# Thirty-two tokens out of the dense expert tiles, and up products with the weights stationary behind all down products

## What is computed

```python
q = (hblk @ w_q).reshape(B, TB, PEER_HEADS, 2, PEER_DHALF)
s = jnp.einsum('btphd,phnd->btphn', q, subkeys)
v, i = lax.top_k(s, PEER_TOPK)                       # 16 of 128 in each half
cand = v[..., 0, :, None] + v[..., 1, None, :]
cidx = i[..., 0, :, None] * PEER_NKEYS + i[..., 1, None, :]
tv, tj = lax.top_k(cand, PEER_TOPK)
eidx = take_along_axis(cidx, tj)
w = jax.nn.softmax(tv, axis=-1)
a = jax.nn.gelu(einsum('btd,btpkd->btpk', hblk, w_down[eidx]))
y = einsum('btpk,btpkd->btd', w * a, w_up[eidx])
x = x + ga2 * y;  out = rms_norm(x, g_norm_final)
```

## Time and profile before

| | us |
|---|---|
| median of three runs | 1717.1 (1715.06 to 1717.36) |
| the profiled execution | 1716.91 |
| its span, first to last instruction | 1715.6 |
| first route step starts on TensorE | 1099.95 |
| last of the 64 route steps ends | 1331.3 |
| the ten pairs end | 1384.4 |
| last up product ends | 1708.8 |
| TensorE busy, share of the span | 98% |
| VectorE busy | 77% |
| ScalarE busy | 56% |
| GpSimd busy | 15% |

### The profile page before, as it was taken

The page is one execution under the profiler, slowest core; times in us unless marked ns, Lnnn a source line. Parts: engine busy times, 40 slices in busy tenths (PEclk is TensorE's granted clock), DMA queues, the critical chain, the costliest instruction groups (busy, mean ns, idle before and its releaser), DMA issues.

```text
span 1715.6 us, 30262 instructions
## 1 busy us (share of the span) xinstructions
PE 1674.8 (98%) x10348; PEld 1496.5 (87%) x10348; DVE 1314.5 (77%) x2590; ACT 956.2 (56%) x1779; POOL 255.6 (15%) x204
## 2 busy tenths in 40 slices
PE   9999999999999999999899999999999999999998
PEld 8888888799988887889899999999989888888886
DVE  5468877867788788867668787799999776666667
ACT  5746554466555544657445554588888543333333
POOL 2120000012100000321117793100010000000000
PEclk9999999999999999999999999999999999999999
DMA  7534767656547677444245558766655555556554
GB/s 241 185 134 154 260 213 273 220 169 211 200 148 274 209 281 257 160 157 144 87 130 193 170 198 310 241 197 196 193 188 168 190 193 190 193 195 195 189 192 146
DMA packets 91674, 336.53 MB, mean 196 GB/s; under 512 B 10305, under 2 KB 10673, under 8 KB 90801
## 3 DMA queue, kind: packets, MB, share of 16 engines
q1 hardware_dynamic: 77328, 279.48, 49.3%
q0 software_dynamic: 7040, 30.20, 5.2%
q10 hardware_dynamic: 7200, 25.45, 3.9%
HBM read 332.94 MB, written 2.13 MB: 195 GB/s over the span
## 4 chain that ended last, share of the span: by engine, by line
PE 52%; DVE 12%; DMA 5%; ACT 4%; issue 3%; POOL 1%; DVEq 0%; SPq 0%; ACTq 0%; POOLq 0%
PE bank L282 12%; PE bank L286 12%; PE bank L283 12%; PE bank L1259 4%; DMA ring<-in_stream 4%; DVE wl L208 4%; ACT wh L201 3%; PE bank L2368 2%; PE bank L1263 2%; PE bank L2371 1%; DVE onehot_j L2686 1%; DVE x L2614 1%; DVE gelu L2387 1%; DVE onehot_i L2685 1%; DMA ada<-in_w_ada 1%
## 5 line engine op out<-in xcount | busy, mean ns | idle before, releaser
L201 ACT ACTIVATE wh<-ring 128x1024 fp32r<-128x1024 f32 x526 | 555.5, 1058 | 560.4 <-PE bank L286 376.6
L208 DVE TENSOR_TENSOR wl<-ring,wh 128x1024 fp32r<-128x1024 f32 x476 | 582.0, 1225 | 274.1 <-ACT wh L201 272.3
L282 PE MATMUL bank<-wh,xs 128*128 128x512 f32 (+1 forms) x852 | 307.6, 361 | 1.9 <-DVE wl L208 0.8
L286 PE MATMUL bank<-wh,xs 128*128 128x512 f32 (+1 forms) x852 | 303.7, 356 | 0.0
L283 PE MATMUL bank<-wl,xs 128*128 128x512 f32 (+1 forms) x852 | 303.4, 356 | 0.0
L282 PE MATMUL bank<-xs,wh 128*128 128x224 f32 (+1 forms) x760 | 214.8, 283 | 4.4 <-DVE wl L208 4.1
L1259 PE MATMUL bank<-xs,wh 128*128 128x512 f32 x672 | 212.4, 396 | 2.5 <-DVE wl L208 2.5
L286 PE MATMUL bank<-xs,wl 128*128 128x224 f32 (+1 forms) x760 | 211.3, 278 | 0.0
L283 PE MATMUL bank<-xs,wh 128*128 128x224 f32 (+1 forms) x760 | 211.2, 278 | 0.0
L2368 PE MATMUL bank<-xs,wh 128*128 128x448 f32 x592 | 189.7, 382 | 0.0
L282 PEld LDWEIGHTS bank<-wh,xs 128*128 128x128 f32 x852 | 160.9, 189 | 28.1 <-DVE wl L208 2.9
(11 more groups left out here) (529 smaller groups left out, 2780.2 us busy)
## 6 DMA issues: line engine op xcount, KB each, us to landing
ring<-in_stream SPq DMA_DIRECT2D x529, 512.0 KB, 3.4
ada<-in_w_ada ACTq DMA_DIRECT2D x48, 512.0 KB, 4.6
rows<-in_rows POOLq DMA_DIRECT2D x1, 2560.0 KB, 11.4
rows<-in_rows POOLq DMA_DIRECT2D x3, 512.0 KB, 5.5
con<-in_early POOLq DMA_DIRECT2D x1, 1374.0 KB, 14.4
x_feature_major<-in_x_fm SPq DMA_DIRECT2D x4, 256.0 KB, 6.3
x<-in_x_tm POOLq DMA_DIRECT2D x1, 1024.0 KB, 5.8
rows<-in_rows POOLq DMA_DIRECT2D x1, 1024.0 KB, 7.0
```

The source lines that it names most:

```text
L201: C.activation(wh[q % AHEAD][:, :], ring[slot][:, :], ACT.Copy).then_inc(s_high, 1)
L208: low.tensor_tensor(wl[q % AHEAD][:, :], ring[slot][:, :], wh[q % AHEAD][:, :], ALU.subtract).then_inc(s_low, 1)
L282: T.matmul(o, left[0], right[0], start=start, stop=False, skip_group_check=True)
L286: return T.matmul(o, left[1], right[0], start=False, stop=stop, skip_group_check=True)
```

## The change

The three groups of edits are these.

- The thirty-two tokens leave the dense work wholly. `ROUTES` falls to 56, `WA` has 224 columns. For their up part, 32 more gathers fetch up rows, from the stream itself. `take_row` is one instruction on DVE for each gathered row set: 32 dots, then (after `factors`: gelu of the dots, times the routing weights) 32 multiply-adds into `own`, which becomes the tokens' result spread over 128 partitions. Takes come in every fifth route step, every third down step behind the routes and every third up step, 64 in all, with two buffers. 16 small matmuls sum over the heads at the end. `x` stays in SBUF.
- `FIRST` falls from 54 to 39, and all downs come before all ups: 39 lead, 56 with a route step, 33 wide downs alone, then 128 ups.
- An up is weight-stationary in the form of the wide down: eight blocks of a matmul with 448 columns and one with 224, into eight PSUM banks. The high part of the weighted activations is made by ACT, the low part by DVE. The result lies by feature, so it is scaled by `ga2` per partition (`result_block`, which also adds the two sides) and transposed back on TensorE before the sum with `x`.

```diff
-FIRST = 54
+FIRST = 39
-BUFS = 3
+BUFS = SETS
-BY_POOL = 28
-ROUTES = S // TB
-LEAD = FIRST + ROUTES
+BY_POOL = 30
+ROUTES = LIVE // TB
+DOWNS = NE - FIRST
+BESIDE_UP = 3
```

```diff
+    def take_row(n):
+        row, r = rows_of[n % BUFS][:, :], n % DOTS
+        mine = own[r // TOPK][:, :]
+        V.wait_ge(s_row[n % BUFS], 16 * (n // BUFS + 1))
+        if n < DOTS:
+            V.tensor_tensor_reduce(out=row, in0=row, in1=mine, ..., accum_out=dots[:, r:r + 1]).then_inc(s_taken, 1)
+        elif r % TOPK == 0:
+            V.tensor_scalar(mine, row, dots[:, r:r + 1], None, ALU.mult).then_inc(s_taken, 1)
+        else:
+            V.wait_ge(s_taken, n)
+            V.scalar_tensor_tensor(mine, row, dots[:, r:r + 1], mine, ALU.mult, ALU.add).then_inc(s_taken, 1)
```

The order of a step with a down tile, in the changed form:

```diff
+    for g in range(DOWNS):
+        if g < ROUTES:
+            route_product(g)
         down_wide(q1 + g, 0, FIRST + g, 0)
         if g + 1 < ROUTES:
             weights_in(g + 1)
         if g >= 1:
             late_gelu(g - 1)
+        if 1 <= g <= ROUTES:
             route_copy(g - 1)
+        if 2 <= g < ROUTES + 2:
             route_multiply(g - 2)
         if g >= 3:
             late_weigh(g - 2)
         if g + 2 < ROUTES:
             onehots(g + 2)
         split(q1 + g + AHEAD)
         late_whole(g)
+        if g % 5 == 2 if g < ROUTES else (g - ROUTES) % 3 == 0:
+            take_row(taken)
+            taken += 1
+    late_gelu(DOWNS - 1)
```

And the ups:

```diff
+    def parts(u):
+        if u >= 3:
+            C.wait_ge(s_used, q2 + u - 2)
+        C.activation(parts_of(u)[:, 0, 0:LIVE], WA[:, u, :], ACT.Copy).then_inc(s_high_part, 1)
+        V.wait_ge(s_high_part, u + 1)
+        V.tensor_tensor(parts_of(u)[:, 1, 0:LIVE], WA[:, u, :], parts_of(u)[:, 0, 0:LIVE], ALU.subtract).then_inc(s_parts, 1)
+    def up_block(u, k, h, l):
+        def both_parts(stop):
+            return T.matmul(sides(k)[:, :, 0:LIVE], h[:, ks], hold[:, :, 0:LIVE], ...)
+        def high_part(stop):
+            return T.matmul(bank[k][:, 0:LIVE], l[:, ks], hold[:, 0, 0:LIVE], ...)
+    for u in range(NE - LATE):
+        up(u)
+        if u + 2 < NE:
+            parts(u + 2)
+        if q2 + u + AHEAD < pieces:
+            split(q2 + u + AHEAD)
+        if u % BESIDE_UP == 1 and taken < 2 * DOTS:
+            if taken == DOTS:
+                factors()
+            take_row(taken)
+            taken += 1
+    parts(NE - 1)
+    T.wait_ge(s_taken, 2 * DOTS)
+    for i in range(SETS):
+        for k in range(KD):
+            T.matmul(sides(k)[:, :, toks], own[i][:, k * P:(k + 1) * P], spread[:, :, :], start=False, stop=True, ...)
+    for k in range(KD):
+        for v in range(LATE):
+            last = up_block(u, k, wh[q % AHEAD], wl[q % AHEAD])
+        if k == 6:
+            for b_ in range(4):
+                result_block(b_)
+            turned_back(0, 0)
+            turned_back(1, 0)
```

More of the change, by code:

```diff
@@ L2292, in build @@
     peer = ExitStack()
-    WA = sb(peer, "weighted", [P, NE, S])
+    WA = sb(peer, "weighted", [P, NE, LIVE])
+    own = [sb(peer, f"own_rows{i}", [P, D]) for i in range(SETS)]
+    rows_of = [sb(peer, f"gathered{i}", [P, D]) for i in range(BUFS)]
     iT = sb(peer, "route_i", [P, S])
@@ new lines, in factors @@
+    def factors():
+        C.wait_ge(s_taken, DOTS)
+        made = act.did(C.activation(dots[:, :], dots[:, :], ACT.Gelu_apprx_tanh))
+        dve.wait(made)
+        V.wait_ge(s_wts_in, 16)
+        made = dve.did(V.tensor_tensor(dots[:, :], dots[:, :], wts[:, :], ALU.mult))
+        V.wait_ge(*made)
+    V.wait_ge(*picked)
+    m = dve.did(V.scalar_tensor_tensor(ups_f, IJ[:, 1, 1].rearrange("p h k -> p (h k)"), float(NE),
+                                       IJ[:, 0, 1].rearrange("p h k -> p (h k)"), ALU.mult, ALU.add))
@@ L2641, in build @@
+    V.wait_ge(*m)
+    numbered_up = dve.did(V.tensor_scalar(ups_of, ups_f, float((pieces - NE) * P), None, ALU.add))
+    V.memset(spread[:, 1, :], 0.0)
+    spread_made = dve.did(V.tensor_reduce(spread[:, 0, :], ident.rearrange("p (t h) -> p t h", h=PH), AX.X, ALU.add))
     act.wait(s1)
@@ L2939, in last_tile @@
-    def last_tile(v, i):
-        n = 0 if i is None else i * BODY
-        u, q = NE - LEAD + v, q2 + v
-        if i is not None or u + 2 < NE:
-            parts(u + 2, n, q, n, last=True)
-        up(q, n, u, n, last=i is not None or v > 0)
-        if i is not None or q + AHEAD < pieces:
-            split(q + AHEAD, i)
-    V.wait_ge(s_weighed, NE - LEAD)
-    parts(NE - LEAD + 1, 0, q2 - 1, 0, last=True)
-    for v in range(BODY):
-        last_tile(v, None)
-    with nc.Fori(1, LEAD // BODY - 1, engines=(ENG.PE, ENG.Activation, ENG.DVE)) as i:
-        for v in range(BODY):
-            last_tile(v, i)
@@ L2955, in build @@
-    ga2_diag = WA[:, 12:16, :].rearrange("p j (a n) -> p (j a) n", a=2)
-    dg2 = diagonals(ga2_diag, 5 * KD)
-    for v in range((LEAD // BODY - 1) * BODY, LEAD - 3):
-        last_tile(v, None)
-        if v == LEAD - 4:
-            ga2, ga2_done = row_of(WA[:, 16:20, :].rearrange("p j t -> p (j t)"), ga2_diag, dg2)
-    parts(NE - 1, 0, q2 + LEAD - 3, 0, last=True)
-    order = [(0, 0, 0), (0, 0, 1), (1, 0, 0), (2, 0, 0), (1, 0, 1), (2, 0, 1), (0, 1, 0), (1, 1, 0), (2, 1, 0),
-             (0, 1, 1), (1, 1, 1), (2, 1, 1)]
@@ new lines, in up @@
+    def up(u):
+        T.wait_ge(s_parts, u + 1)
+        def products(h, l):
+            for k in (0, 1, 2, 3, 7, 4, 5, 6):
+                if u == 0 and k == 0:
+                    T.wait_ge(s_wc, ROUTES)
+                    T.wait_ge(s_wm, ROUTES)
+                if u == 0 and k == 4:
+                    T.wait_ge(s_whole, DOWNS)
+                last = up_block(u, k, h, l)
+            return last
+        piece_ops(q2 + u, 0, products)
+    for u in range(2):
+        parts(u)
+    late_weigh(DOWNS - 2)
@@ new lines, in build, with result_block @@
+    for i in range(SETS):
+        toks = slice(LIVE + i * GROUP, LIVE + (i + 1) * GROUP)
+        for k in range(KD):
+            T.matmul(sides(k)[:, :, toks], own[i][:, k * P:(k + 1) * P], spread[:, :, :], start=False, stop=True,
+                     skip_group_check=True)
+    result = flat[:, 7168:9216].rearrange("p (k t) -> p k t", k=KD)
+    right = flat[:, 9216:10240].rearrange("p (i t) -> p i t", t=S)
+    block_done, right_in, block_in, summed_up = {}, {}, {}, {}
+    def result_block(k):
+        col = mod[:, 5 * KD + k:5 * KD + k + 1]
+        act.wait(block_done[k], block_in.get(k - 4))
+        right_in[k] = act.did(C.activation(right[:, k % 4, :], bank[k][:, S:2 * S], ACT.Copy, scale=col))
+        V.wait_ge(*right_in[k])
+        block_in[k] = dve.did(V.scalar_tensor_tensor(result[:, k, :], bank[k][:, 0:S], col, right[:, k % 4, :], ALU.mult, ALU.add))
```

346 lines of the change are left out of this document (119 added, 227 removed).

## The result

| | before | after |
|---|---|---|
| median of seven runs each, us | 1715.06 (1711.76 to 1717.36) | 1704.67 (1700.52 to 1708.48) |
| ratio after / before | | 0.9939, 95% interval 0.9925 to 0.9954 |
| the profiled execution, us | 1716.91 | 1708.48 |
| its span | 1715.6 | 1707.2 |
| first route step starts | 1099.95 | 1052.05 |

The kernel got 10.4 us faster, where 23 were forecast: the sign was right, but more than half of the gain is missing.

The account below looks back on a forecast made before the run. TensorE, busy for 98% of the span, was taken to bound the kernel. Start of the routes -46.9, route steps -31.9, downs and pairs +47.5, ups with their ends +7.0, tail +1.1 gave 1694 us, range 1679 to 1713.

Parts of the forecast that it names:

- The ring between ACT and DVE: In the lone downs, gelu, high half, low half and sum wait for each other in turn: 2.95 us a step, above TensorE's 2.51.
- The first route step: First step behind the lead: keeps its 5.10 us, since the second one-hot matrices still come behind the lead.
- The summing matmuls, last ups and transposes: Behind the wait for all takes: 2.7 us for 16 summing matmuls, 7.5 for three ups, 1.8 for eight transposes.
- a rival with the clock: In the ups, idle moments between eight banks lower the clock to 1.2 GHz in one of ten: 31 us more, 1725; 2%.
- The idle time before the first up: Between lone downs and ups, TensorE waits 3.7 us for low half, sum, gelu, high part and both parts.
- The lone downs: Thirty-three wide downs behind the route steps: 2.5 + 32 x 2.95 = 96.9 us until the last split begins.
- The ups: Ups ahead of the last take's wait: 2.51 us each instead of 2.72, 125 in 313.8 us, plus 2 us for loads.
- The tail: From the last product to the end of the span: 7.9 us instead of 6.8, bounds 7 and 10.
- Ups that don't get shorter: Rival: writing eight banks in turn costs TensorE what it gains, an up stays at 2.72, 27 us more, 1720; 7%.
- A slot of three late: Rival: in the ups the load that meets the gather always lands after 5.6 us, 2.67 us a step, 1712; 14%.
- all loads slow: Rival: loads in the ups land after 6.4 us on the mean, 2.94 us a step, 54 us more, 1745; 7%.
- The missing ring: Rival: ACT and DVE don't hold the 33 lone downs, which run at 2.51 us, 14 us less, 1680; 10%.

Follow-up runs that it names:

- no_takes_in_the_ups: The changed kernel with the 42 gathers and takes of the ups left out, so the thirty-two tokens get no right result: 1697.48 us, ratio 0.9881 to before.
- end_without_wait: The changed kernel with takes in the ups one step earlier, last ups reordered and summing matmuls by twos between their blocks: 1695.74 us, ratio 0.988 to before.
- lead_of_54: The changed kernel with 54 tiles of lead again instead of 39, and five takes more in the ups: 1707.89 us, ratio 0.9948 to before.
- all_four: The changed kernel with lone downs' gelu behind the next high half, early parts for the first ups, end without its wait, tail result blocks earlier: 1682.11 us.

## Why the prediction was right and wrong

**What held.** The route steps took 198.4 us against 199.5; a take costs about 0.5 there. They began 1.1 us earlier than I had said: six transposes took some 0.5 us and not 1.4. The ring between ACT and DVE bound the lone downs at 2.93 to 2.97 us against 2.95, and taking it apart proved it. The wait for the last take was 3.65 us against 3.6. The loads hardly showed in the ups. These terms were added up from rows of the same instructions.

**What held by luck.** The first route step took 5.14 us against 5.10, but the 5.10 of before were something else. There TensorE worked through the whole step at a lower clock, and the step would have been 3.4 long at full clock. In after it took 3.58 us at a clock of 1.00, with 1.56 us of waiting for the second one-hot matrix behind it:

```profile
1052.05:1055.60 3.55, 3.55 (x26) 3.19 (x24) 2.20 (x3) 1.30 (x2) 0.00 (x0) 1.00 0.65 216
```

The summing matmuls, last ups and transposes, 12.0 us in the sum, would have come out near it at full clock because two errors cancel: the row of summing matmuls takes 3.5 and not 2.7, and eight transposes take 0.8 (1694.96 to 1695.75 in after) and not 1.8. The transposes had been priced at 0.225 each, by a row of matmuls that are no transposes.

**The step that failed: idle time of TensorE was priced as itself only.** The sum had both idle times, 3.7 us before the first up and 3.6 before the summing matmuls, at their own length, and the work behind them at full speed. The row that speaks against it was in the trace of before. There TensorE waits 2.46 us for a one-hot matrix, and the windows that follow show a lower clock, which I took for the first step's own length:

```profile
1099.95:1101.80 1.85, 1.85 (x13) 1.80 (x14) 0.92 (x1) 1.13 (x2) 0.68 (x2) 0.87 0.53 111
1101.80:1105.20 3.40, 3.40 (x15) 3.17 (x14) 2.71 (x5) 1.28 (x4) 1.16 (x1) 0.57 0.83 280
1105.20:1110.00 4.80, 4.80 (x38) 4.64 (x37) 2.92 (x5) 4.44 (x11) 0.00 (x0) 1.00 0.47 159
```

A stretch at a lower clock loses (1 - clock) x its length, for work that TensorE does without a pause: here 0.24 + 1.46 = 1.7 us. Read from this row, the two new idle times would have added 3.4 us to the sum. In after the falls lasted longer, 3.0 us behind the first and 6.3 us behind the second. So the row of before would have given the mechanism and about a third of its size. For the first idle time the cause is shown: with matmuls put into it, and with the gap closed, the clock stayed at 1.00. At the end idle time is only part of it, since the row of narrow matmuls costs clock without any (1.7 us in `no_takes_in_the_ups`). I did have a rival with the clock, but put it at the eight banks and gave it 2%. The banks were innocent: the granted clock is 1.00 over 310 us of ups that go through all eight in every step. The section that I had cited, A second HAM failure mode: psum-queue depth-cycling, in the Trainium skill's page TensorE: Matmul & The Clock Gate, describes something that no run here shows. The section of the same page that bore on this case is HAM oscillation — how this bites in real kernels, which says that idle gaps bring the clock down and that the work behind them starts cold. The trace agrees: 0.50 behind 6.74 and behind 3.65 us of idle time, and 1.00 behind the first once it was filled or closed. The fall without idle time in `no_takes_in_the_ups` (0.56 over 3.85 us) goes beyond what that section says.

**The terms that were mis-sized.**

- *The idle time before the first up*, 6.74 us against 3.7. The 3.7 are right for the chain behind the last split (1350.66 to 1354.44, 3.78 us). But TensorE doesn't wait for that split, which is of a piece for the ups. It ended its last down one ring step (2.97 us) earlier, at 1347.70. That made the idle time longer without moving the first up.
- *The lone downs*, 3.4 us longer: six steps took 3.2 to 3.9 us instead of 2.95, three of them with a take and a late piece; ACT waited 1.7 us for loads, the rest I didn't separate.
- *The ups*, +4.8: 3.0 by the clock in the first two, 123 x 0.025 = 3.1 by the pitch (2.535, not 2.51), against 2 us set for the loads, of which 0.7 came.
- *The summing matmuls and the last ups*, +4.2 and +2.1, together 6.3 by the clock. At full clock both cost together about what the forecast said (11.5 us for the last window of `end_without_wait`, which holds the sums between blocks and the ups), by the two errors told above. Taken singly, the sums were 0.8 too cheap, and 3.4 came by the clock.
- *The tail*, 10.25 against 7.9. I had credited 0.85 us for DVE's backlog. What came instead is that all blocks of the result are needed before any token's last half is done, so all four stores stand at the very end. In before SP began its four 0.2 us ahead of the last product's end and issued them over 5.11 us; here it began 6.0 us behind it and issued them within 2.32:

```profile
1708.59 5.11 SPq L3035 DMA_DIRECT2D out<-weighted  x4
```

```profile
1702.93 2.32 SPq L2980 DMA_DIRECT2D out<-weighted  x4
```

**The rivals.** Ups that don't get shorter: no, 2.72 became 2.53. A slot of three late, or all loads slow: no, one landing took 7.7 us but the median was 4.1, and 23 waits of ACT ended in 0.7 us of idle PE. The missing ring: no in after, yes as an experiment, where the stage became 13.1 us shorter, of the 14 that I had said, and the whole 10.2. The clock in the ups: it cost 3.0 us in the first two, by the idle time ahead of them and not by the banks.

**Left open.** Why the profiled execution is 3.8 us above the median of its kind (its mean clock is 0.987, that of the other six 0.989 to 0.991, so a longer time at the lower level is likely, but only one execution has a trace). How the end's 9 us shrank to 5.2 beside the other edits: gaps before late pieces were seen, but not why they fell there. How the 6.3 us of lower clock at the end divide between the idle time and the row of narrow matmuls. Which part of the tail's 2.4 us belongs to the stores alone.

## What to carry to other kernels

A wait of TensorE can cost its length and then the half speed of what comes behind it, and so can a row of narrow matmuls: before a wait of a few us is put into a sum, look for a wait of that kind in the trace at hand and read the granted clock of the windows behind it. When the order of a stage is changed, ask at its seam how far TensorE runs ahead of the other engines, since that distance becomes its idle time; cheap work put into the seam (here the parts of the first ups, or even matmuls of no use) wins more than its own time. And once a ring or a wait is gone, the next bound stands close behind it, here the loads: of a promised sum of gains a part comes back.

## What the runs showed of the hardware

- After 6.74 and 3.65 us of idle time the granted clock stood at 0.50 for about 6 and 12 us of work, though TensorE was busy all the while. After a gap of 2.46 us (before) the loss of 1.7 us makes some 3.4 us at 0.50, and the clock was 0.66 on the mean over the 5.0 us after a gap of 2.02 us (`lead_of_54`). The gaps of 1.78 us and less in `all_four` had no such trace (1.00 in the windows behind them), nor had one of 2.14 us in before (1.00 from 768.2 to 772.8, with TensorE busy for 2.6 of these 4.6 us). So the length of a gap alone doesn't tell whether the clock falls.
- A row of 32 recorded matmuls with 32 columns each, 3.50 us with no idle time ahead of it, ran at 1.00 and was followed by 0.56 over 3.85 us (`no_takes_in_the_ups`).
- A float32 product with 128x128 weights and 32 columns takes 0.18 us at full clock between other matmuls, 0.22 in a row (3.50 / 16), and 0.43 us at 1.2 GHz in a row. A 128x128 transpose takes 0.10 (0.79 / 8). A block of a 448-column and a 224-column matmul takes 0.317 us (2.535 / 8) at full clock and 0.59 at 1.2 GHz.
- The formula for the isolated gap in the section Back-to-back issue gap of the Trainium skill's page TensorE: Matmul & The Clock Gate made an up 2.28 us, an estimate; measured were 2.53, with or without gathers beside it.
